# RWKV-7 recurrence of a two-layer encoder: four 64x64 tiles of TensorE, the levels' identity as a matmul, and the key factors on ScalarE

## What is computed

```
k = k * (1.0 + (a - 1.0) * k_a)
kk = heads(k0 * k_k);  kk = kk * rsqrt(max(sum(kk * kk), 1e-24))
for each token t:
    sk = state @ kk_t
    state = state * w_t - sk (x) (kk_t * a_t) + v_t (x) k_t
    y_t = state @ r_t
```

## Time and profile before

| | us |
|---|---|
| median of 3 runs | 2944.93 (2935.22 to 2945.01) |
| the profiled execution | 2938.78 |
| its span | 2937.0 |
| PE busy | 2683.2 (91%) |
| DVE busy | 1589.4 (54%) |
| POOL busy | 1246.0 (42%) |
| ACT busy | 948.4 (32%) |

### The profile page before, as it was taken

The page is one execution under the profiler, slowest core; times in us unless marked ns, Lnnn a source line. Parts: engine busy times, 40 slices in busy tenths (PEclk is TensorE's granted clock), DMA queues, the critical chain, the costliest instruction groups (busy, mean ns, idle before and its releaser), DMA issues. The chain is left out here.

```text
span 2937.0 us, 51498 instructions
## 1 busy us (share of the span) xinstructions
PE 2683.2 (91%) x21600; PEld 2204.9 (75%) x21600; DVE 1589.4 (54%) x2030; ACT 948.4 (32%) x1615; POOL 1246.0 (42%) x630
## 2 busy tenths in 40 slices
PE   1878888999999999989999599999799999999999
PEld 1565667788887788767777488888787888788887
DVE  5754454665553633366865478888435333333334
ACT  2434433322214222244544233343334222222221
POOL 2532224544435444444344335444356444444443
PEclk9989999999999999999999899999999999999999
DMA  6421224345442222237566444444232222223223
GB/s 242 154 93 37 86 83 154 128 174 172 165 136 86 94 100 101 94 102 187 156 172 158 115 97 98 95 95 87 89 122 86 101 97 97 87 93 108 94 100 122
DMA packets 299013, 341.94 MB, mean 116 GB/s; under 512 B 214560, under 2 KB 214688, under 8 KB 298784
## 3 DMA queue, kind: packets, MB, share of 16 engines
q1 hardware_dynamic: 298784, 338.65, 37.3%
HBM read 297.77 MB, written 39.85 MB: 115 GB/s over the span
## 5 line engine op out<-in xcount | busy, mean ns | idle before, releaser
L709 POOL TENSOR_TENSOR wl<-w,wh 128x1024 fp32r<-128x1024 f32 x367 | 902.3, 2465 | 1278.6 <-ACT wh L750 1278.3
L180 PE MATMUL ps<-hi,wh 128*128 128x512 f32 x2208 | 884.6, 401 | 21.7 <-ACT qk_raw L787 10.0
L181 PE MATMUL ps<-lo,wh 128*128 128x512 f32 x2208 | 869.8, 394 | 0.0
L182 PE MATMUL ps<-hi,wl 128*128 128x512 f32 x2208 | 869.3, 394 | 0.0
L750 ACT ACTIVATE wh<-w 128x1024 fp32r<-128x1024 f32 x367 | 386.9, 1056 | 684.3 <-DMA w<-in_ffn_w_in 523.0
L1021 DVE SCALAR_TENSOR_TENSOR xt<-ps,mod,xt 128x512 f32<-128x512 f32 x384 | 286.4, 749 | 425.2 <-PE ps L182 417.8
L180 PEld LDWEIGHTS ps<-hi,wh 128*128 128x128 f32 x2208 | 420.9, 191 | 124.9 <-issue 33.6
L181 PEld LDWEIGHTS ps<-lo,wh 128*128 128x128 f32 x2208 | 421.4, 191 | 90.3 <-issue 3.7
L182 PEld LDWEIGHTS ps<-hi,wl 128*128 128x128 f32 x2208 | 420.2, 190 | 90.2
L1026 DVE TENSOR_TENSOR act<-ps,silu 128x512 f32<-128x512 f32 x88 | 60.8, 691 | 482.2 <-PE ps L182 482.2
L180 PE MATMUL ps<-act_hi,wh 128*128 128x512 f32 x704 | 282.3, 401 | 16.4 <-DVE act_lo L1030 9.7
(11 more groups left out here) (225 smaller groups left out, 3443.2 us busy)
## 6 DMA issues: line engine op xcount, KB each, us to landing
w<-in_ffn_w_in SPq DMA_DIRECT2D x176, 512.0 KB, 3.3
piece<-in_ada_w SPq DMA_DIRECT2D x96, 512.0 KB, 5.0
w<-in_ffn_w_out SPq DMA_DIRECT2D x88, 512.0 KB, 3.3
w<-in_w_rkv SPq DMA_DIRECT2D x48, 512.0 KB, 3.8
scratch<-silu SPq DMA_DIRECT2D x48, 256.0 KB, 3.0
scratch<-act SPq DMA_DIRECT2D x48, 256.0 KB, 2.8
w<-in_wqk SPq DMA_DIRECT2D x20, 512.0 KB, 4.7
xt<-in_xT SPq DMA_DIRECT2D x4, 2048.0 KB, 11.8
```

What stands on the lines that cost most here:

```text
L180: pe.matmul(out, w_hi(k), x_hi(k), start=first and k == 0, stop=False)
L181: pe.matmul(out, w_hi(k), x_lo(k), start=False, stop=False)
L182: ins = pe.matmul(out, w_lo(k), x_hi(k), start=False, stop=last and k == kc - 1)
L709: pool.tensor_tensor(wl[n % NW][:, :, :], wr[n % NW][:, :, :], wh[n % NW][:, :, :].bitcast(F32), ALU.subtract).then_inc(*wlo.up)
```

## The change

What it does: (1) `heads` yields a second slice `away`, which for the upper four pairs is the other half, and visits pairs i and i+4 together, so that four matmuls in a row lie in four tiles. Most products read `hs` and write `away`, or the reverse; those with the state, the transposed level product and `by_feature` stay in their half. (2) The chunk's sums go into half banks 3 and 4, and `solve_x` is split into `known_x` (no state) and the state part; `outputs` and `state_products` become one block, with the state's terms last. (3) A level's identity is 16 more matmuls in the same PSUM sum, and ACT copies the result out: `level` leaves DVE. (4) ACT makes both key factors: 8 scales of 64 columns by k_k, and 8 of `a` by k_a plus (1 - k_a); POOL multiplies by k once, in place of two operations. `begin` leaves DVE. (5) `centre` has two operations in place of three, and comes after `new_state`, which now comes ahead of `products_b`. (6) In the front, `rope` has 9 operations in place of 18 and cosine is taken of |angle|; the first weights are loaded after the conditioning pieces.

```diff
+                def away(j, h):
+                    return home(j, h if j < QP else 1 - h)
-                def heads(j0, j1):
-                    for j in range(j0, j1):
-                        for h in range(2):
-                            yield j, slice(h * HEAD, (h + 1) * HEAD)
+                def heads(pairs=PAIRS):
+                    for i in range(pairs // 2):
+                        for j in (i, i + pairs // 2):
+                            for h in range(2):
+                                yield j, home(j, h), away(j, h)
...
ACT
+                        def keys(ch):
+                            act.wait_ge(*g["tiles_in"].at(3 * ch + 3))
+                            act.wait_ge(*g["kb_done"].at(ch))
+                            act.wait_ge(*g["rk_done"].at(ch))
+                            for j in range(PAIRS):
+                                ins = act.activation(kk[:, j, :], kt_[:, j, :], ACT.Copy, scale=vec[:, V_KK + j:V_KK + j + 1])
+                            ins.then_inc(*g["kk_done"].up)
+                            for j in range(PAIRS):
+                                ins = act.activation(k2[:, j, :], at_[:, j, :], ACT.Identity, scale=vec[:, V_KA + j:V_KA + j + 1],
+                                                     bias=rest[:, j:j + 1])
+                            ins.then_inc(*g["t1_done"].up)
+                        def level(ch, l):
+                            act.wait_ge(*g["x_done_w"].at(NL * ch + l + 1))
+                            act.activation(in_two(wx[l % 2]), two_banks(0), ACT.Copy).then_inc(*g["w_done"].up)
                             if l < NL - 1:
+                                act.wait_ge(*g["tr_done"].at(NT * ch + 2 * l + 1))
+                                act.activation(in_two((tinv, tdiag[ch % 2])[l]), two_banks(0), ACT.Copy).then_inc(*g["t_done"].up)
+                            act.wait_ge(*g["tr_done"].at(min(NT * ch + 2 * l + 2, NT * (ch + 1))))
+                            act.activation((tinv_t, tdiag_t[ch % 2], inv[ch % 2])[l][:, :, :], bank(2), ACT.Copy).then_inc(*g["t_done"].up)
...
                             if zz is not None:
                                 root(zz)
                             if w is not None:
-                                squares(w)
+                                keys(w), squares(w)
                             if x is not None:
                                 token_out(x, 1)
...
PE
+                            for j, to, hs in heads():
+                                pe.matmul(spot(0, j, to), idst[hs], idst[hs], start=j % QP == 0, stop=False)
+                            for j, to, hs in heads():
+                                ins = pe.matmul(spot(0, j, to), ntm[l][ch % len(ntm[l])][hs, j, :], (tdiag[ch % 2], tinv, tdiag[ch % 2])[l][hs, j, :],
+                                                start=False, stop=j % QP == QP - 1)
...
                         def period(w, x, d, y, zz, zp):
                             if zz is not None:
-                                solve_x(zz)
+                                known_x(zz)
                             if zp is not None:
                                 by_feature(zp)
+                            if zz is not None:
+                                solve_x(zz)
...
                             if zz is not None:
-                                outputs(zz)
+                                outputs_and_state(zz)
                             if x is not None:
                                 gram(x, 0)
-                            if zz is not None:
-                                state_products(zz)
...
DVE
                             if zz is not None:
-                                centre(zz)
+                                new_state(zz), centre(zz)
                             if x is not None:
-                                products_b(x)
-                            if zz is not None:
-                                new_state(zz)
-                            if x is not None:
-                                decayed_keys(x)
-                            if w is not None:
-                                begin(w)
+                                products_b(x), decayed_keys(x)
```

More of the change, by code:

```diff
@@ L75 @@
 C_GNEPS = C_EPS + 1
-C_END = C_GNEPS + 1
+C_HALFPI = C_GNEPS + 1
+C_END = C_HALFPI + 1
 C_RESET = C_END
@@ L634, in _ @@
                         for step, *e in plan.order:
-                            if step == "part" and e[1] == 0:
+                            if step == "part" and e[1] == 0 and tiles[e[0]][0] == "ada" and tiles[e[0]][-1] == 1:
+                                pass
+                            elif step == "part" and e[1] == 0:
                                 load(top[e[0]] + AHEAD + 1)
@@ L1658, in level_t @@
+                            pe.wait_ge(*g["t_done"].at(NT * ch + 2 * l))
+                            if l == 0:
+                                pe.wait_ge(*tt_in[ch % 2].at(4 * (ch // 2 + 1)))
+                            if l < NL - 1:
+                                for j, hs, to in heads():
+                                    ins = pe.matmul(spot(0, j, to), old[hs, j, :], wx[l % 2][hs, j, :], start=True, stop=True)
                                 ins.then_inc(*g["tr_done"].up)
-                        def solve_x(ch):
+                            for j, hs, _ in heads():
+                                ins = pe.matmul(bank(2)[hs, j, :], wx[l % 2][hs, j, :], old[hs, j, :], start=True, stop=True)
@@ L1669, in solve_x @@
+                        def solve_x(ch):
+                            pe.wait_ge(*g["s_done"].at(ch))
+                            pe.wait_ge(*g["x_known"].at(ch + 1))
+                            for j, hs, _ in heads():
+                                ins = pe.matmul(spot(3, j, hs), ar[ch % (RING + 1)][hs, j, 0, :], state[hs, j, :], start=False, stop=j % QP == QP - 1)
                             ins.then_inc(*g["xs_done"].up)
@@ new lines, in outputs_and_state @@
+                            ins.then_inc(*g["y_known"].up)
+                            for j, hs, _ in heads():
+                                if j < QP:
+                                    pe.matmul(spot(3, j, hs, HALF // 2), ar[ch % (RING + 1)][hs, j, 1, :], state[hs, j, :], start=False, stop=j % QP == QP - 1)
+                            pe.wait_ge(*g["y_known"].at(ch + 1))
+                            for j, hs, _ in heads():
+                                if j >= QP:
+                                    ins = pe.matmul(spot(3, j, hs, HALF // 2), ar[ch % (RING + 1)][hs, j, 1, :], state[hs, j, :], start=False, stop=j % QP == QP - 1)
```

194 lines of the change are left out of this document (81 added, 113 removed).

## The result

The kernel with the change takes **3033.09 us** (median, 3026.66 to 3035.06), the one before, on the same chip, 2940.55: a ratio of 1.031 (1.028 to 1.033). It is slower, as forecast, but by 43 us more than forecast, and just above the range of 2905 to 3028. The profiled execution has a span of 3030.0 us, against 2937.0.

The account below looks back on a forecast made before the run. PE was taken as the bound, DVE close behind; after the change, a chain through PE, ACT and DVE. 2938.8 + 70 (12 full periods) + 8 (filling) - 8 (emptying) - 19 (front) = 2990 us, range 2905 to 3028.

Parts of the forecast that it names:

- Rival E: Recurrence: the chain is hidden by chunks in flight, DVE sets the pace, 21.7 us a period, 2865 us; chance 0.16.
- D: ACT's key operations cost only 0.12 us each, chain 26.8 us a period, clock holds, 2926 us; chance 0.12.
- B: PE's clock holds despite two stalls a period: 29.1 us a period, 2954 us; chance 0.17.
- Rival C: Four tiles start no faster at 64 columns: +2.9 us a period, 3025 us; chance 0.10.
- emptying: The 5 emptying periods have no keys and keep part of PE's gain: -8 us, 1.5 each.
- front: Up to the first large product: half the angle operations, DVE done 16 us sooner, 3 for a DMA wait: -19 us.
- the price of TensorE: Four-tile matmuls of 64 columns on PE: 0.031 us each, in place of 0.059 in two tiles.
- steps 5 and 6: ACT takes u, 0.7 us; then PE's `outputs_and_state`, 64 matmuls at 0.031 us, 3.15 us in all.
- Step 4: The level's copy on ACT, then PE's `level_t` and `solve_u`, to ACT: 2.95 us, PE idle about 3 us.
- Step 3: ACT takes x and goes through seven more operations before it is free for the level: 3.8 us.
- Step 10: ACT's 16 key operations, `keys(w)`, ahead of the squares: 4.2 us, bounds 1.9 and 5.5.
- Step 7: DVE: `new_state` and `centre` 2.65 us, five masks 2.99, `decayed_keys` 0.8: 6.4 us.

Follow-up runs that it names:

- experiment 1: Changed kernel with ACT's eight scales for the removal factor moved behind the squares and the copy of k_tok: 2987.72 us, 1.018 of the kernel before.
- experiment 2: Changed kernel with five 128x512 filler products on PE ahead of its wait for the squares in `norms`: 3005.14 us, 1.024.
- experiment 9: Changed kernel with the levels' identity as two wide PE products a level in place of 16 small ones, copies staying on ACT: 3011.89 us, 1.026.
- the control: The changed kernel itself, run again beside a rerun with one added PE product on the chain: 3031.78 us, 1.031.
- Experiment 8: Changed kernel with the levels' identity back on DVE, one operation a level replacing ACT's copy and 16 matmuls: 3001.49 us, 1.021.
- experiment 13: The kernel of experiment 10 with the third level's DVE operation moved ahead of `begin(w)` and `variance(zz)`: 2943.21 us, 1.001.
- experiment 5: Changed kernel with the loads of k, a and the decay waiting for `chunk_used` as well: 3030.13 us, 1.030.
- experiment 10: Changed kernel with keys back on DVE and POOL and the levels' identity back on DVE; four tiles, order and front kept: 2944.92 us, 1.001.

## Why the prediction was wrong

The direction and the mechanism hold: in the recurrence PE's work fell, a chain through ACT took its place, the clock fell behind the stall. Rival E (DVE sets the pace) and D (cheap keys) fall with experiment 1, B (the clock holds) with the clock of 0.86 and experiment 2. Rival C's 3025 us is the nearest number of all, but by luck: its slower start of a record is refuted by the 14.7 ns. The size failed. Against my sum:

| us | forecast | measured |
|---|---|---|
| 12 periods | +70 | +89 (407.0 - 318.3) |
| filling | +8 | +5 |
| emptying | -8 | +9 |
| front | -19 | -12.5 |
| behind the recurrence | 0 | +3 |

**The step that failed is the price of TensorE**, 0.031 us a matmul wherever one stood, and with it steps 5 and 6 and the emptying. The price itself was right: 0.029 us (two records of 14.7 ns) where a burst runs. But it holds for a burst only. Where stalls follow each other the instructions come at about 30 ns a record, and experiment 9, with fewer instructions and more work, is faster. At that pace PE's 802 records of a period (9620 / 12) need 24 us, more than the 17.9 that I counted. In the period shown, step 5 took 1.66 us for 0.7 and step 6 5.02 for 3.15: 2.8 us more, of which 0.75 and 1.74 are the two stalls. That the stalls are there, and that I had put them at nothing, is measured. That they are the supply rests on the count of records and on experiment 9. I had weighed rival C, a slower start of a record, and rejected it by the earlier trace rows; what I didn't ask is whether 32 records at that pace say anything of 700. The emptying, where I gave PE's gain back as -8, is for the most part the same error: PE's issue waits there are 11.9 us, 1.4 before, which is 10.5 of the 17 us missed.

**Step 4 and the clock.** I charged 1.7 + 1.3 us for half clock. The first stall costs 1.9 (experiment 2). Behind the second, 2.13 us long, the clock was still 1.00 in the period shown and 0.50 in others, as the busy time by stretch has it (columns as in the second fence; the first two rows are of the period shown, the third of another one):

```profile
1907.00:1911.00 4.00, 1.87 (x109) 1.73 (x103) 2.13 (x2) 3.18 (x8) 3.46 (x3) 1.00 0.00 0
...
1932.00:1938.00 6.00, 4.55 (x62) 2.97 (x64) 2.20 (x9) 1.88 (x5) 0.00 (x0) 0.51 0.53 125
...
1809.50:1812.50 3.00, 3.00 (x106) 3.00 (x104) 1.80 (x2) 1.45 (x3) 1.68 (x2) 0.50 0.45 116
```

Seven of the 12 periods have such a second stretch of some 3.5 us at half clock: five behind this wait, two behind issue stalls of 2.27 and 2.31 us. So "may not always bring the clock down" was right. But it costs little: the seven periods last 34.0 us on average, the other five 33.8 (in the control's trace 33.9 for ten, 33.3 for two). That is 0.1 to 0.5 us a period in place of 1.3, and the rest hid a part of the error above. The stalls' lengths were forecast at 5 and 3 us, and measured 5.7 and 2.1.

**Step 3 and 4**, ACT's queue ahead of the level's copy, were right: 3.82 us for 3.8, 2.80 for 2.95. Experiment 8 shows what that placement costs. Step 10, the keys: 4.56 for 4.2. Its upper bound was added up wrongly: with the 0.11 us for eight of them it is 6.3 us, not 5.5. The sum doesn't use it. **Step 7** came out at 6.39 for 6.4, and yet it misled: I costed the masks only on the chain through DVE. The blocks' way through DRAM starts at the first mask, and once the keys are gone PE waits for it in every period (experiment 13). In the changed kernel it is hidden.

**The front.** DVE was free of angles at 21.3 us (21 forecast), and the last conditioning sum ended at 51.03, 15.6 us sooner than 66.63. So the 3 us that I had counted for the last piece's wait did not come. Then 3.1 us were lost: in `t` at 55.06, two operations take 4.78 us in place of 1.41, while POOL splits the weights (51.88 to 59.29), which it did before while DVE was waiting (the first row is of the kernel before):

```profile
70.66 1.41 DVE L1164 SCALAR_TENSOR_TENSOR t<-xt,gain,squares 128x512 f32<-128x512 f32 x2 [0.20 <-DVE mod L1038]
...
55.06 4.78 DVE L1164 SCALAR_TENSOR_TENSOR t<-xt,gain,squares 128x512 f32<-128x512 f32 x2 [0.20 <-DVE mod L1041]
...
51.88 7.41 POOL L711 TENSOR_TENSOR wl<-w,wh 128x1024 fp32r<-128x1024 f32 x3 [15.13 <-ACT wh L752]
```

Both the 3 us and "from the last piece's start to the first large product, unchanged" were wrong. That the two engines disturb each other is read from their overlap, and was not tried by itself.

Left open: what sets the 3.8 us of an instruction block (experiment 5 moved the nearest loads away and changed little), why neighbouring stalls are up to 4.9 us apart in some places, why experiment 8's issue waits did not fall with its records, and how much of the 2.8 us of steps 5 and 6 a full supply would give back, as no run took the stalls away entirely. How much of the 16 us by which experiment 10 lags the kernel before, once the front is taken off, is the order and how much the supply was not separated.

## What to carry to other kernels

Twice the pace in a burst is not twice the work: for long runs of small matmuls in straight-line code, count the instructions and compare with the pace at which they arrived in the trace, here about 30 ns a record, before costing a faster tiling. Fewer, wider products can win although the engine works longer on them (experiment 9). Look at the clock and the stalls in all periods, as one period can be the exception. And when work moves to an idle engine, look at its place in that engine's queue: ACT was idle for half of the time, but not at the two points where the chain passed.

## What the runs showed of the hardware

- Four 64x64 tiles start a float32 record of 64 columns every 14.7 ns (32 in 0.47 us), at full clock.
- At that pace PE stalls with no releaser, mostly after 127 or 128 matmul records with their weight loads, and neighbouring stalls end 3.5 to 4.9 us apart. At 29 ns a record there were 1.1 us of such stalls in 12 periods, at 14.7 ns 27.4 us.
- The granted clock was at half behind stalls of 5.7 us and in most periods behind ones of 3.2, behind single ones of 2.27, 2.31 and 2.38 us, and behind five waits of 2.13 to 2.14 us. Behind six other waits of that length it stayed at full. A filler of 4.56 us, with a wait of 1.25 us behind it, kept it at full for `norms` and `by_feature`.
- An ACT operation of 64 columns starts 0.25 us after the last with one per-partition operand (2.00 us for eight), and 0.33 with two.
